# Hybrid encoder trunk: both mixing stages in a new order, small parameters loaded first, and two additions of each state-space tile moved from VectorE to GpSimd

## The chip, the cores and the metric

The kernel runs on one core of a Trainium2 chip. The time is the device time of one execution in microseconds (us). The five engines of the core run side by side, each through its own instruction stream in order: TensorE (PE, matrix products into PSUM banks), VectorE (DVE), ScalarE (ACT), GpSimd (POOL) and SyncE (SP, which here only starts DMAs). They wait for one another by semaphores.

## The reference

The input is 256 tokens of 1024 features, in float32. After a layer norm come two layers. Each has a token mixer and then a channel mixer, and each ends with a residual sum and a layer norm. The channel mixer is a dense SwiGLU in layer 0 and a top-2-of-8 mixture of experts in layer 1.

The token mixer projects the tokens once and hands the columns to four head groups of 256 features: retention, S5 (a diagonal state-space model), Hyena (gated long convolutions, whose filters come from a small sine network) and mLSTM. Their outputs are concatenated and projected. The S5 part is

```python
bu = einsum("gpc,blgc->blgp", b_bar[direction], ug)
_, states = associative_scan(combine, (decay, bu), reverse=reverse, axis=1)   # a_bar is complex
return einsum("gcp,blgp->blgc", c[direction], states).real
y = run(0, False) + run(1, True) + d_skip * u
z = gelu(y);  out = z * sigmoid(z @ w_glu)
```

## The kernel before

The kernel is written by hand, engine by engine. Each engine's part has a function `mix_0` for the mixer of layer 0 and `mix_1` for that of layer 1, which list the calls in the order in which that engine runs them. Nothing is planned by a program: the lists are the schedule. Between the two mixers stands the dense channel mixer (products at L1030 and L1040), and behind the second one the experts (L1145, L1172), which take up the time from about 600 us to the end.

**The projection.** The input projection is cut into 12 units (`unit`, L616). Unit 0 gives the S5 inputs, units 1 to 3 the Hyena columns, 4 and 5 the query and key columns of the mLSTM, 6 and 7 those of retention, 8 to 11 the remaining ones. Each is 8 or 16 products over the 1024 features (L640 or L648). `UNITS` gives their order and `WIN_LOADS` the weight transfers that bring them in pairs. Units 4 and 5 come last before the change. The output projection (`out_product`, L846) accumulates four banks over the four head groups.

**The state-space tiles.** The complex scan is made real by rotating the inputs by the phase of each state and back. There are eight tiles of 128 states, each with both directions, and per tile these steps:

- TensorE: `s5_in` (L784) multiplies B and the inputs into one PSUM bank, real and imaginary halves. It uses 32 rows of the array.
- VectorE: `s5_tile_products` (L2009, L2010) multiplies a table of cosines and sines by the two halves of the bank: two instructions of 1024 elements per partition, one input in SBUF, the other in PSUM. The scratch tiles are `p1` and `p2`.
- VectorE: `s5_tile_scan` first completes the rotation (an addition at L2019 and a subtraction at L2020, 512 elements, both inputs in SBUF), then runs four scans of 256 elements (L2025, L2027).
- VectorE: `s5_tile_rotate` (L2038, L2039, L2041) turns the states back.
- GpSimd: adds the two parts (L521, 1024 elements), straight after the rotation. When four tiles are done TensorE multiplies them by C (`s5_y`, L807).

**The other work on VectorE.** In layer 0 VectorE and ScalarE also build the tables (`pre(0, 13)` to `pre(0, 20)`, one for each tile, L1822 to L1830), the S5 constants (`s5_angle`, `pre(0, 11)`, `pre(0, 12)`) and the Hyena filters (`pre(0, 0)` to `pre(0, 6)`; TensorE's part at L587 and L600). In layer 1 all of that is done during the dense channel mixer, and the tables are loaded. `conv` (L1837, L1842) is the short convolution, `rotary`, `ml_rows_a`, `ml_rows_b`, `hyena_product`, `hyena_gate` (L1889, L1893), `ret_decay` and `ret_norm` serve the other groups.

**The tail.** After retention's head norm the mLSTM is left: `ml_mask` (L1958), an exponential on ScalarE, `ml_weights`, `ml_out` on TensorE for each of four heads, then `ml_norm`, `head_scale(1)`, a transpose (`head_out`, L688) and the last output products. In both layers the first `ml_mask` of VectorE marks the start of this tail.

**Parameters.** `pr` holds the small parameters and the weights of one layer, 1728 KB, loaded by one DMA (SP, L416) behind the inputs, the norm weights, the identity and the first weights of the projection. The semaphore `s_par` covers all of it.

`link` makes VectorE wait for its own last result before the next instruction.

## Time and profile before

| | us |
|---|---|
| median of 3 runs | 1611.61 (1609.13 to 1612.51) |
| the profiled execution | 1607.81 |
| its span | 1606.0 |

The times of engines over the span: PE 1562.5 busy (97%), DVE 1337.2 (83%), ACT 963.7 (60%), POOL 47.1 (3%). A busy PE isn't a PE at its peak, since its records overlap. The page cuts the span into 40 slices; each digit is a share in tenths:

```profile
PE   7998999999999899999999999999999999999997
DVE  6999567766498867889989998988998989898897
ACT  3321455644212346777777677677777777777775
POOL 0112000000021100000000000000000000000000
PEclk9998999999999999999999999999999999999999
```

A slice is 40 us. The mixer of layer 0 fills slices 1 to 5, that of layer 1 the end of slice 11 to slice 15. POOL works in these two only.

### The profile page before, as it was taken

To read this page: it belongs to the slowest core of one execution; us is meant where nothing else is said; L and a number is where in the kernel's file an instruction comes from. 1 tells how busy PE (TensorE), PEld (TensorE's weight loads), DVE (VectorE), ACT (ScalarE), POOL (GpSimd) and SP (SyncE) were. 2 spreads that over 40 slices of the span, in tenths; PEclk is the share of its full clock that TensorE was granted. 3 is DMA by queue.
4 is the path that set the end of the run, shared out by engine and by line. 5 is a ranking of instruction groups with operands and counts; after the bars stand their busy time and mean duration, and the time that the engine had idled before them with its cause. 6 is when DMAs were issued, how large, how long until landed. Compare 5 with 4: busy or idle time off the path is not lost.

```text
span 1606.0 us, 18396 instructions
## 1 busy us (share of the span) xinstructions
PE 1562.5 (97%) x7492; PEld 1235.9 (77%) x7492; DVE 1337.2 (83%) x1435; ACT 963.7 (60%) x1000; POOL 47.1 (3%) x34
## 2 busy tenths in 40 slices
PE   7998999999999899999999999999999999999997
PEld 5656679988766667888888888888888788888885
DVE  6999567766498867889989998988998989898897
ACT  3321455644212346777777677677777777777775
POOL 0112000000021100000000000000000000000000
PEclk9998999999999999999999999999999999999999
DMA  8231445644424156999889999989899989999981
GB/s 334 105 133 52 157 159 231 245 174 171 193 105 142 61 230 274 372 369 379 342 341 370 355 369 371 354 333 372 345 378 373 348 343 368 380 361 373 365 338 52
DMA packets 41676, 446.33 MB, mean 278 GB/s; under 512 B 4457, under 2 KB 4585, under 8 KB 8433
## 3 DMA queue, kind: packets, MB, share of 16 engines
q1 hardware_dynamic: 39360, 438.78, 70.2%
q10 hardware_dynamic: 2224, 6.31, 1.1%
q8 instruction: 61, 1.00, 0.2%
q14 instruction: 31, 0.25, 0.0%
HBM read 439.81 MB, written 5.26 MB: 277 GB/s over the span
## 4 chain that ended last, share of the span: by engine, by line
PE 80%; DVE 13%; ACT 4%; issue 1%; DMA 1%; POOL 0%; SPq 0%; DVEq 0%; ACTq 0%
PE bank L1145 35%; PE bank L1172 16%; PE bank L1030 8%; PE bank L640 4%; PE bank L1040 4%; PE bank L648 3%; PE bank L846 3%; DVE ring_lo L2198 2%; PE bank L1153 1%; DVE ring_lo L2340 1%; ACT ex_up_hi L1498 1%; PE bank L1093 1%; DMA pr<-par 1%; PE bank L1116 1%; ACT ex_w_hi L1624 1%
## 5 line engine op out<-in xcount | busy, mean ns | idle before, releaser
L2198 DVE TENSOR_TENSOR ring_lo<-ring,ex_up_hi 128x2048 fp32r<-128x2048 f32 x224 | 512.9, 2290 | 51.3 <-ACT ex_up_hi L1498 49.8
L1498 ACT ACTIVATE ex_up_hi<-ring 128x2048 fp32r<-128x2048 f32 x224 | 429.2, 1916 | 105.9 <-PE bank L1145 105.9
L1145 PE MATMUL bank<-ex_up_hi,ex_x_hi 128*128 128x512 f32 x896 | 362.6, 405 | 5.6 <-DVE ring_lo L2198 4.7
L1145 PE MATMUL bank<-ring_lo,ex_x_hi 128*128 128x512 f32 x896 | 350.7, 391 | 0.0
L1145 PE MATMUL bank<-ex_up_hi,ex_x_lo 128*128 128x512 f32 x896 | 349.7, 390 | 0.0
L2340 DVE TENSOR_TENSOR ring_lo<-ring,ex_w_hi 128x2048 fp32r<-128x2048 f32 x111 | 253.2, 2281 | 0.0
L1624 ACT ACTIVATE ex_w_hi<-ring 128x2048 fp32r<-128x2048 f32 x111 | 211.5, 1905 | 0.0
L1145 PEld LDWEIGHTS bank<-ex_up_hi,ex_x_hi 128*128 128x128 f32 x896 | 168.3, 188 | 43.8 <-DVE ring_lo L2198 12.3
L1145 PEld LDWEIGHTS bank<-ring_lo,ex_x_hi 128*128 128x128 f32 x896 | 168.2, 188 | 36.7
L1145 PEld LDWEIGHTS bank<-ex_up_hi,ex_x_lo 128*128 128x128 f32 x896 | 168.8, 188 | 30.5
L1172 PE MATMUL bank<-ex_w_hi,ex_mid_hi 128*128 128x512 f32 x448 | 174.5, 389 | 0.0
L1172 PE MATMUL bank<-ring_lo,ex_mid_hi 128*128 128x512 f32 x448 | 174.3, 389 | 0.0
L1172 PE MATMUL bank<-ex_w_hi,ex_mid_lo 128*128 128x512 f32 x448 | 174.3, 389 | 0.0
L1172 PEld LDWEIGHTS bank<-ex_w_hi,ex_mid_hi 128*128 128x128 f32 x448 | 84.1, 188 | 17.7 <-DVE ring_lo L2340 0.3
L1172 PEld LDWEIGHTS bank<-ring_lo,ex_mid_hi 128*128 128x128 f32 x448 | 84.1, 188 | 17.5
L1172 PEld LDWEIGHTS bank<-ex_w_hi,ex_mid_lo 128*128 128x128 f32 x448 | 84.1, 188 | 17.4
L1030 PE MATMUL bank<-ff_x_hi,ff_up_hi 128*128 128x256 f32 x336 | 96.1, 286 | 0.0
L1030 PE MATMUL bank<-ff_x_hi,ff_up_lo 128*128 128x256 f32 x336 | 95.1, 283 | 0.0
L1030 PE MATMUL bank<-ff_x_lo,ff_up_hi 128*128 128x256 f32 x336 | 95.1, 283 | 0.0
L1618 ACT ACTIVATE sc<-bank 128x256 f32<-128x256 f32 x112 | 43.0, 384 | 84.2 <-PE bank L1145 84.2
L648 PE MATMUL bank<-win,hT 128*128 128x512 f32 x192 | 93.4, 619 | 0.0
L640 PE MATMUL bank<-hT,win 128*128 128x256 f32 x384 | 85.4, 381 | 3.1 <-ACT hT L1247 1.6
(355 smaller groups left out, 2028.1 us busy)
## 6 DMA issues: line engine op xcount, KB each, us to landing
ring<-moe SPq DMA_DIRECT2D x112, 2048.0 KB, 7.6
ring<-moe SPq DMA_DIRECT2D x112, 1024.0 KB, 7.4
ring<-ffn SPq DMA_DIRECT2D x11, 3072.0 KB, 11.1
win<-w_in SPq DMA_DIRECT2D x12, 2048.0 KB, 8.6
win<-w_out SPq DMA_DIRECT2D x4, 2048.0 KB, 10.2
lnb<-ln SPq DMA_DIRECT2D x4, 1024.0 KB, 5.7
tab<-yT ACTq DMA_DIRECT2D x8, 512.0 KB, 5.5
pr<-par SPq DMA_DIRECT2D x2, 1728.0 KB, 11.1
```

The lines of the kernel that those rows point to most:

```text
L640: ins = mm(b[:, half * L:(half + 1) * L], w[:, k, c:c + P], hT[:, k, :], start=(k == 0), stop=(k == KT - 1))
L648: ins = mm(b[:, :], x, w[:, k, :], start=(k == 0), stop=(k == KT - 1))
L846: ins = mm(bank[b][:, :], yT[:, k, t * P:(t + 1) * P], w[:, k, :], start=(n == 0 and i == 0), stop=(n == 3 and i == 1))
L1030: ins = mm(bank[4 + u % 2][:, w * L:(w + 1) * L], (ff_up if u else ff_up_first)[j][:, w, k, :], ff_x[i][:, k, :], start=(k == 0 and n == 0 ...
L1040: ins = mm(bank[2 * t + hf][:, :], ff_mid[i][:, u % 2, t * P:(t + 1) * P], w2[j][:, hf * 512:(hf + 1) * 512], start=False, stop=(u == NU - ...
L1145: ins = mm(b[:, :], ex_x[x % 3][x_][:, k, :], (ex_up_hi, lo)[w_][:, k, :], start=(k == 0 and m == 0), stop=(k == KT - 1 and m == 2))
L1172: ins = mm(bank[2 * (x % 2) + hf][:, :], ex_mid[a][:, g % 2, f * P:(f + 1) * P], w2[b], start=(c == 0 and f == 0 and m == 0), stop=(c == N ...
L1498: act(ex_up_hi[:, HS * q:HS * (q + 1), :], wt[:, HS * q:HS * (q + 1), :], ACT.Copy).then_inc(e_uh, 1)
L1618: act(sil[g % 2], bank[4 + g % 2][:, 0:L], ACT.Silu).then_inc(e_sil, 1)
L1624: act(ex_w2_hi[g % 2][:, :], ring[here][:, UPW:SLOT], ACT.Copy).then_inc(e_wh, 1)
L2198: tt(ring_lo[s][:, half], ring[s][:, half], hi.bitcast(F32), ALU.subtract).then_inc(e_ul, 1)
L2340: tt(ring_lo[s][:, UPW:SLOT], ring[s][:, UPW:SLOT], ex_w2_hi[g % 2][:, :].bitcast(F32), ALU.subtract).then_inc(e_wl, 1)
```

## The change

- GpSimd does the addition and subtraction of L2019 and L2020. Its loop now runs nine times: in turn `i` it waits for the products of tile `i`, completes them, and only then sums the rotated states of tile `i - 1`. VectorE's scan waits for the new semaphore `b_in`.
- `s5_in` serves several tiles in one call, each into a bank of its own (four at once in layer 1, two and two in layer 0), and alternates between the row groups of the array.
- The second and third layer of the filter network use both halves of the rows: the weights `hy_w2` and `hy_w3` are laid out twice and side by side, and the products of one token tile come in pairs. The squares of the filters in layer 0 are added on VectorE first (`square_total(0)`), so that TensorE needs 4 products in place of 16 for the norm.
- The columns of `pr` from `gate_b` on (the S5 constants, biases and norm weights) come in a DMA of their own, before all others, with the semaphore `s_small`. The small constants (`cst`, behind the identity) come before the first projection weights; the rest of `pr` comes behind these. `s5_angle(0)` on VectorE and `s5_step(0)`, `s5_radius(0)`, `pre(0, 11)` on ScalarE move ahead of the first layer norm.
- The units run in the order 0, 8, 9, 10, 11, 1 to 7, always through banks 5 and 6, and all engines have new lists in both mixers. The semaphores of the weight slots for the dense and expert parts are merged into one for each slot.

```diff
-UNITS = (0, 8, 9, 10, 11, 1, 2, 3, 6, 7, 4, 5)
+UNITS = (0, 8, 9, 10, 11, 1, 2, 3, 4, 5, 6, 7)
 POS = {u: p for p, u in enumerate(UNITS)}
-UNIT_BANK = (5, 6, 5, 6, 5, 6, 5, 6, 5, 6, 1, 2)
 VW = H * (HD + 1)
-WIN_LOADS = ((0, (0, 3)), (1, (8, 9)), (2, (10, 11)), (1, (1, 2)), (2, (6, 7)), (0, (4, 5)))
+WIN_LOADS = ((0, (0, 1)), (1, (8, 9)), (2, (10, 11)), (1, (2, 3)), (0, (4, 5)), (2, (6, 7)))
...
-    ("s5_c", 2 * 16 * 32), ("s5_b", 512), ("glu", 512), ("hy_w3", 1024), ("hy_w12", 64), ("gate_w", KT * 16),
+    ("s5_c", 2 * 16 * 32), ("s5_b", 512), ("glu", 512), ("hy_w3", 960), ("hy_w12", 128), ("gate_w", KT * 16),
...
-        fx_ = [[a[0:64, i * 256:(i + 1) * 256] for i in range(4)] for a in work]
+        fx_ = [[a[:, i * 256:(i + 1) * 256] for i in range(4)] for a in work]
...
 
+        def s5_bank(l, i):
+
+            if l:
+                return i if i < 4 else 3
+            return 2 + i % 2 if i < 4 else 3
...
                     sp.wait_ge(f_pm, 2)
-                    sp.wait_ge(f_sq, 4)
+                    sp.wait_ge(f_sq, 5)
                 elif n == 4:
...
                 sp.dma_start(ln_home(n), ln[n]).then_inc(s_ln, 16)
 
+            few = PAR["gate_b"][0]
+            sp.dma_start(pr[:, few:PAR_W], par[0, :, few:PAR_W]).then_inc(s_small, 16)
             for t in range(TT):
                 sp.dma_start(h[:, t, :], x[t * P:(t + 1) * P, :]).then_inc(s_x[t], 16)
             load_ln(0)
             first = slice(*CONST["ident"])
             sp.dma_start(cst[:, first], const[:, first]).then_inc(s_id, 16)
+            sp.dma_start(cst[:, first.stop:CONST_W], const[:, first.stop:CONST_W]).then_inc(s_pos, 16)
...
                 ins.then_inc(ml_ones, 1)
-                for i in range(8):
-                    po.wait_ge(b_x, 2 * (8 * l + i + 1))
-                    T = s5_table(i)
-                    nc.gpsimd.tensor_tensor(T, T, s5_work[2 + i % 2], ALU.add).then_inc(b_sum, 1)
+                p1, p2 = s5_work[0:2]
+                for i in range(9):
+                    if i < 8:
+                        po.wait_ge(b_p, 8 * l + i + 1)
+                        nc.gpsimd.tensor_tensor(p1[:, 0], p1[:, 0], p2[:, 1], ALU.add).then_inc(b_in, 1)
+                        nc.gpsimd.tensor_tensor(p2[:, 0], p2[:, 0], p1[:, 1], ALU.subtract).then_inc(b_in, 1)
+                    if i:
+                        po.wait_ge(b_x, 2 * (8 * l + i))
+                        T = s5_table(i - 1)
+                        nc.gpsimd.tensor_tensor(T, T, s5_work[2 + (i - 1) % 2], ALU.add).then_inc(b_sum, 1)
                 for m in range(2):
...
-                elif k < 6:
-                    j = k - 2
-                    if j == 0:
+                    mm(pb[1][:, 0:L], W("hy_w12", 64), fx[3][0:64], start=True, stop=True).then_inc(f_mm, 1)
+                elif k in (3, 5):
+                    pass
                         pe.wait_ge(f_sin, 2 * l + 2)
-                    if j >= 2:
-                        pe.wait_ge(f_win, 4 * l + j - 1)
-                    mm(pb[j % 2][:, :], fx[3][:, (j // 2) * P:(j // 2 + 1) * P],
-                       W("hy_w3", 64)[:, (j % 2) * 512:(j % 2 + 1) * 512], start=True, stop=True).then_inc(f_raw, 1)
+                    else:
+                        pe.wait_ge(f_win, 4 * l + 2)
+                    for o in range(2):
+                        r = slice(64 * o, 64 * o + 64)
+                        mm(pb[o][:, :], fx[3][r, t * P:(t + 1) * P], W("hy_w3")[r, 0:512],
+                           start=True, stop=True).then_inc(f_raw, 1)
                 elif k == 6:
-                    if l:
-                        pe.wait_ge(f_sq, 5)
-                        terms = [(0, 0)]
-                    else:
-                        pe.wait_ge(f_win, 4)
-                        pe.wait_ge(f_sq, 2)
-                        terms = [(t, d) for t in range(TT) for d in range(2)]
+                    pe.wait_ge(f_sq, 3 * l + 3)
                     for j in range(4):
                         o, c = j // 2, j % 2
-                        for i, (t, d) in enumerate(terms):
-                            ins = mm(pb[0][:, 2 * j:2 * j + 2], fsq[t][:, o, d, c * P:(c + 1) * P], K("ones")[:, 0:2],
-                                     start=(i == 0), stop=(i == len(terms) - 1))
+                        ins = mm(pb[0][:, 2 * j:2 * j + 2], fsq[0][:, o, 0, c * P:(c + 1) * P], K("ones")[:, 0:2],
+                                 start=True, stop=True)
...
-            def s5_in(l, i):
-
-                if i == 0:
+            def s5_in(l, first, n):
+
+                if first == 0:
                     pe.wait_ge(s_par, 16 * (l + 1))
                     pe.wait_ge(u_ev, l + 1)
                 else:
-                    pe.wait_ge(b_p, 8 * l + i)
-                r = 32 * (i % 4)
+                    pe.wait_ge(b_p, 8 * l + first)
                 for s in range(2):
-                    ins = mm(bank[3][:, s * L:(s + 1) * L], s5b[r:r + 32, i // 4, s, :],
-                             uT[r:r + 32, i // 4, :], start=True, stop=True)
-                ins.then_inc(b_mm, 1)
+                    for i in range(first, first + n):
+                        r = 32 * (i % 4)
+                        ins = mm(bank[s5_bank(l, i)][:, s * L:(s + 1) * L], s5b[r:r + 32, i // 4, s, :],
+                                 uT[r:r + 32, i // 4, :], start=True, stop=True)
+                        if s:
...
-            def square_total():
-
-                fsq = fsq_[1]
-                ve.wait_ge(f_sq, 4)
+            def square_total(l):
+
+                fsq = fsq_[l]
+                ve.wait_ge(f_sq, 3 * l + 2)
...
                 p1, p2 = s5_work[0:2]
-                ve.wait_ge(b_p, v + 1)
-
-                tt(p1[:, 0], p1[:, 0], p2[:, 1], ALU.add)
-                link(tt(p2[:, 0], p2[:, 0], p1[:, 1], ALU.subtract))
```

VectorE's list in layer 0, and below it the part of layer 1 from tile 4 on (tiles 0 to 3 stay as they were: products, scan and rotation one after the other, with `gates(1)` before the second rotation):

```diff
             def mix_0():
-                s5_angle(0)
                 pre(0, 11)
-                pre(0, 12)
                 pre(0, 13)
                 pre(0, 14)
                 pre(0, 15)
+                ve.wait_ge(ht_ready, 4)
+                pre(0, 12)
+                s5_tile_products(0, 0)
+                s5_tile_scan(0, 0)
                 pre(0, 16)
+                s5_tile_rotate(0, 0)
                 pre(0, 17)
-                s5_tile_products(0, 0)
+                s5_tile_products(0, 1)
                 pre(0, 18)
-                s5_tile_scan(0, 0)
-                gates(0)
-                s5_tile_rotate(0, 0)
-                pre(0, 19)
-                pre(0, 20)
-                s5_tile_products(0, 1)
                 s5_tile_scan(0, 1)
                 s5_tile_rotate(0, 1)
                 pre(0, 0)
+                gates(0)
                 s5_tile_products(0, 2)
+                s5_tile_scan(0, 2)
                 pre(0, 1)
-                conv(0, 1)
-                s5_tile_scan(0, 2)
-                conv(0, 2)
                 s5_tile_rotate(0, 2)
                 s5_tile_products(0, 3)
+                pre(0, 19)
+                pre(0, 20)
+                s5_tile_scan(0, 3)
+                conv(0, 1)
+                s5_tile_rotate(0, 3)
+                conv(0, 2)
+                s5_tile_products(0, 4)
                 pre(0, 2)
-                conv(0, 3)
-                s5_tile_scan(0, 3)
                 pre(0, 3)
-                s5_tile_rotate(0, 3)
                 pre(0, 4)
-                s5_tile_products(0, 4)
                 pre(0, 5)
                 s5_tile_scan(0, 4)
+                square_total(0)
+                s5_tile_rotate(0, 4)
+                conv(0, 3)
+                conv(0, 4)
+                s5_tile_products(0, 5)
                 pre(0, 6)
-                s5_tile_rotate(0, 4)
                 pre_norm(0)
-                ml_rows_a(0)
-                rotary(0, 6)
-                s5_tile_products(0, 5)
-                ml_rows_b(0)
-                rotary(0, 7)
                 s5_tile_scan(0, 5)
                 s5_tile_rotate(0, 5)
                 s5_tile_products(0, 6)
+                ml_rows_a(0)
+                s5_tile_scan(0, 6)
+                ml_rows_b(0)
+                conv(0, 5)
+                s5_tile_rotate(0, 6)
+                s5_tile_products(0, 7)
+                hyena_product(0, 0)
                 ml_cols(0)
-                hyena_product(0, 0)
-                s5_tile_scan(0, 6)
+                s5_tile_scan(0, 7)
+                rotary(0, 6)
+                rotary(0, 7)
+                hyena_gate(0, 0)
+                s5_tile_rotate(0, 7)
                 ret_decay(0, 0)
                 ret_decay(0, 1)
-                s5_tile_rotate(0, 6)
-                s5_tile_products(0, 7)
-                hyena_gate(0, 0)
-                s5_tile_scan(0, 7)
-                s5_tile_rotate(0, 7)
+                hyena_product(0, 1)
                 ret_decay(0, 2)
                 ret_decay(0, 3)
-                hyena_product(0, 1)
+                s5_skip(0)
                 ret_norm(0)
-                s5_skip(0)
-                conv(0, 4)
+                hyena_gate(0, 1)
                 head_scale(0)
-                conv(0, 5)
-                hyena_gate(0, 1)
                 ml_mask(0, 0)
                 ml_mask(0, 1)
-                s5_end(0)
                 ml_weights(0, 0)
                 ml_weights(0, 1)
                 ml_mask(0, 2)
+                ml_mask(0, 3)
                 ml_weights(0, 2)
-                ml_mask(0, 3)
+                s5_end(0)
                 ml_weights(0, 3)
                 ml_norm(0)
...
                 s5_tile_scan(1, 4)
                 s5_tile_rotate(1, 4)
                 conv(1, 2)
+                s5_tile_products(1, 5)
                 conv(1, 3)
+                s5_tile_scan(1, 5)
                 ml_rows_a(1)
-                s5_tile_products(1, 5)
-                hyena_product(1, 0)
-                ml_rows_b(1)
-                rotary(1, 6)
-                hyena_gate(1, 0)
-                ml_cols(1)
-                s5_tile_scan(1, 5)
                 s5_tile_rotate(1, 5)
                 s5_tile_products(1, 6)
-                rotary(1, 7)
-                hyena_product(1, 1)
-                ret_decay(1, 0)
+                ml_rows_b(1)
+                conv(1, 4)
+                conv(1, 5)
                 s5_tile_scan(1, 6)
                 s5_tile_rotate(1, 6)
+                hyena_product(1, 0)
+                ml_cols(1)
+                s5_tile_products(1, 7)
+                rotary(1, 6)
+                s5_tile_scan(1, 7)
+                rotary(1, 7)
+                hyena_gate(1, 0)
+                s5_tile_rotate(1, 7)
+                ret_decay(1, 0)
                 ret_decay(1, 1)
-                s5_tile_products(1, 7)
-                conv(1, 4)
-                s5_tile_scan(1, 7)
-                s5_tile_rotate(1, 7)
+                hyena_product(1, 1)
                 ret_decay(1, 2)
                 ret_decay(1, 3)
-                hyena_gate(1, 1)
-                conv(1, 5)
                 s5_skip(1)
                 ret_norm(1)
+                hyena_gate(1, 1)
                 head_scale(2)
+                s5_end(1)
                 ml_mask(1, 0)
-                s5_end(1)
+                ml_mask(1, 1)
                 ml_weights(1, 0)
-                ml_mask(1, 1)
                 ml_weights(1, 1)
                 ml_mask(1, 2)
+                ml_mask(1, 3)
                 ml_weights(1, 2)
-                ml_mask(1, 3)
                 ml_weights(1, 3)
                 ml_norm(1)
```

TensorE in layer 0 runs `s5_in(0, 0, 2)` behind unit 0, `s5_in(0, 2, 2)` behind unit 10, and one tile at a time from the fifth on. `pre(0, 6)`, with its new wait for `square_total(0)`, stands ahead of unit 5, `pre(0, 7)` to `pre(0, 10)` inside it. Units 6 and 7 come last, and behind them `hyena_inverse(0, 0)`, retention, `s5_y(0, 1)` and the output products. In layer 1 `s5_in(1, 0, 4)` stands in the middle of unit 8, as `s5_in(1, 0)` did.

## Rows read from the trace of the kernel before

**Rows 1.** Windows by stage: span, busy us (instructions) of PE, PEld, DVE, ACT, POOL; clock; DMA.
```profile
36.00:174.20 138.20, 131.55 (x551) 87.89 (x550) 124.90 (x197) 40.38 (x66) 20.50 (x9) 0.93 0.23 84
174.20:213.80 39.60, 36.81 (x135) 19.21 (x135) 23.08 (x57) 17.29 (x39) 1.65 (x1) 1.00 0.60 231
438.40:557.40 119.00, 113.62 (x524) 77.55 (x524) 105.11 (x164) 25.71 (x42) 20.56 (x9) 1.00 0.27 98
557.40:594.30 36.90, 36.79 (x129) 19.86 (x130) 23.50 (x56) 15.63 (x35) 1.65 (x1) 0.95 0.52 200
```
**Rows 2.** DVE's waits, layer 0 mixer (36 to 174.2 us): total, times, longest.
```profile
DVE cv L1837 <- ACT cv L1311: 9.9, 3, 4.4
```
**Rows 3.** DVE's waits, layer 1 mixer (438 to 557.4 us).
```profile
DVE cv L1837 <- ACT cv L1311: 7.1, 3, 4.0
DVE ring L1930 <- ACT ring L1350: 2.7, 1, 2.7
DVE lnb L1910 <- POOL small L524: 1.8, 1, 1.8
```
**Rows 4.** Timeline of DVE, layer 1, tile 0: start, us, instruction.
```profile
438.40 1.22 DVE L2009 TENSOR_TENSOR ring<-ring,bank 128x1024 f32<-128x1024 f32 x1 [14.78 <-PE bank L793]
...
440.79 0.69 DVE L2019 TENSOR_TENSOR ring<-ring 128x512 f32<-128x512 f32 x1
...
442.11 1.27 DVE L2025 TENSOR_TENSOR_SCAN ring<-small,ring 128x256 f32<-128x256 f32 x2
...
447.17 1.22 DVE L2009 TENSOR_TENSOR ring<-ring,bank 128x1024 f32<-128x1024 f32 x1
```
**Rows 5.** POOL's instructions by line: busy, mean ns, idle before.
```profile
L521 POOL TENSOR_TENSOR ring<-ring 128x1024 f32<-128x1024 f32 x16 | 37.8, 2359 | 231.0 <-DVE ring L2041 231.0
```
**Rows 6.** Single DVE lines: duration in ns, least/median/most.
```profile
L1760 DVE TENSOR_SCALAR sc<-sc x2: 284/1126/1967, 61.6 to 67.8; 64x256 f32<-64x256 f32 x2
L1822 DVE TENSOR_SCALAR yT<-cst,small x16: 341/349/2543, 26.9 to 50.8; 128x256 f32<-128x256 f32 x16
L1930 DVE TENSOR_SCALAR ring<-ring x2: 416/1436/2457, 105.6 to 496.5; 4x512 f32<-4x512 f32 x2
L1893 DVE TENSOR_TENSOR yT<-cv x2: 691/704/717, 173.4 to 546.8; 128x512 f32<-128x512 f32 x2
```
**Rows 7.** Timeline of POOL and DVE: two sums, and what ran beside the second.
```profile
105.42 2.35 POOL L521 TENSOR_TENSOR ring<-ring 128x1024 f32<-128x1024 f32 x1 [10.12 <-DVE ring L2041]
...
544.59 2.36 POOL L521 TENSOR_TENSOR ring<-ring 128x1024 f32<-128x1024 f32 x1 [8.64 <-DVE ring L2041]
...
546.78 0.72 DVE L1893 TENSOR_TENSOR yT<-cv 128x512 f32<-128x512 f32 x1
```
**Rows 8.** Timeline of DVE at the start; idle time before and its releaser in brackets.
```profile
17.94 0.17 DVE L1748 TENSOR_TENSOR small<-pr,small 128x16 f32<-128x16 f32 x1 [4.22 <-ACT small L1255]
...
20.94 0.18 DVE L1785 TENSOR_TENSOR small<-small 128x16 f32<-128x16 f32 x1 [2.11 <-ACT small L1283]
...
23.04 0.69 DVE L1805 TENSOR_TENSOR yT<-pr,small 128x512 f32<-128x512 f32 x1
...
26.90 0.62 DVE L1822 TENSOR_SCALAR yT<-cst,small 128x256 f32<-128x256 f32 x2
...
28.74 0.62 DVE L1822 TENSOR_SCALAR yT<-cst,small 128x256 f32<-128x256 f32 x2
...
36.02 1.21 DVE L2009 TENSOR_TENSOR ring<-ring,bank 128x1024 f32<-128x1024 f32 x1
```
**Rows 9.** Timeline of SP at the start: the norm's DMA.
```profile
1.66 0.42 SPq L408 DMA_DIRECT2D lnb<-ln  x1
```
**Rows 10.** Timeline of DVE: a short convolution (its first half).
```profile
163.20 0.87 DVE L1837 SCALAR_TENSOR_TENSOR cv<-bank,pr,cv 128x255 f32<-128x255 f32 x2 [4.36 <-ACT cv L1311]
```
**Rows 11.** Timeline of PE: 64-row products, in one row group and in two by turns.
```profile
176.78 1.13 PE L760 MATMUL bank<-cv 64*128 64x256 f32 x8
...
348.06 1.12 PE L587 MATMUL bank<-pr,cv 64*128 64x512 f32 x2
```

296 lines of the change are left out of this document (152 added, 144 removed).

## The prediction

> **What bounds the kernel now.** I began with the chain of waits over the whole span, to see which part belongs to TensorE alone. The dense part and the experts are a chain of PE products, and the change gives them almost nothing. What it touches is the two mixers, so I cut these out as windows [rows 1]. In the mixer of layer 0, from the first product of a state-space tile to the first `ml_mask`, DVE is busy for 124.9 of 138.2 us, and PE's clock is granted at 0.93: PE has to wait often enough to lose it, and DVE sets the pace. In layer 1 the two are closer: PE is busy for 113.6 of 119.0 us, DVE for 105.1. There DVE's own waits [rows 3] are mostly for columns that PE hasn't projected yet. Behind the first `ml_mask` both layers run a tail of fixed length, 39.6 and 36.9 us [rows 1]: four heads of mLSTM, its norm, the last output products. So the question for each mixer is when DVE reaches that mask. The timeline of DVE, POOL and PE inside the windows gives the prices.
>
> **What POOL does to DVE.** This decides the case. In three places a TENSOR_SCALAR of DVE runs beside POOL's sum, and takes 1967, 2543 and 2457 ns where the same line otherwise takes 284, 349 and 416 [rows 6]. It waits until POOL is done; the three stalls are 5.9 us. The products of a tile, one input in SBUF and one in PSUM, run beside the sum at their usual 1.22 us [rows 4]. An instruction with both inputs in SBUF meets the sum just once: L1893 begins at 546.78, POOL ends at 546.95 [rows 7], and that instance takes 717 ns, against 691 for the same line elsewhere [rows 6]. The TENSOR_SCALARs come free some 0.14 us before POOL's recorded end (L1930 from 105.6 for 2457 ns, less its usual 416, is 107.6; that sum ends at 107.8 [rows 7]), and 546.95 less 0.14 less 546.78 is 0.03 us: what L1893 has lost. One instance of 26 ns is thin, but it is the only row, and it says that two SBUF inputs are held back as well. The scans (L2025), the rotation (L2038 to L2041), `pre(0, 6)` and `ml_rows_b` are all of that kind.
>
> The Trainium skill says the same, and it speaks against this change: in SBUF — State Buffer, section "Who interferes with whom", a DVE instruction with two SBUF inputs contends with a GpSimd instruction that reads SBUF, and whichever comes second is blocked whole. By that page the sum is the first one below; without it, by the products' row alone, it would be the rival's.
>
> **The change, part by part.**
>
> *Two instructions leave DVE.* From L2019 to the first scan is 1.32 us [rows 4], eight tiles a layer: 10.6 us less of DVE in each.
>
> *What takes their place.* The scan now waits for POOL. Its price for 512 elements isn't shown. The nearest row is its own 1024-element sum, 2359 ns [rows 5]; half of that, 1.18, is the lower end, the whole of it the upper. I take 1.23, since time per element is what the larger one mostly shows, and 0.1 for the two hand-overs: 2.56 us a tile (2.4 to 4.8), 20.5 a layer. Behind the waiting scan stands all of DVE's list. What DVE does between products and scan can cover it only where it has an input in PSUM. In layer 0 that is `pre(0, 2)` to `pre(0, 5)` and the first four instructions of `hyena_product(0, 0)`, each time four of 0.6 us, 4.9 together. The other fillers there are TENSOR_SCALARs. In layer 1 it is `conv(1, 1)` and `conv(1, 3)` at 1.7 (two halves of 0.87, [rows 10]), the start of `rotary(1, 6)` at 1.3, and I give 1.5 for `conv(1, 4)` and `conv(1, 5)`: 6.2. Tiles 0 to 3 of layer 1 have nothing between.
>
> *The sum moves.* Before, it started with the rotation's end and lay beside the next tile's products, which it leaves alone. Now it comes behind POOL's new pair, and so beside the scans of the next tile. If these are held back, it costs 2.36 us for each tile but the last: 16.5 a layer. If not, nothing.
>
> *The start.* DVE waits 4.2 us, until 17.9, for the parameters by way of ScalarE, and 2.1 for ScalarE's sines [rows 8]. With the small ones first, both waits hide in front of and behind the first norm. One more DMA issue (0.42 us, [rows 9]) delays the norm by 0.4. So: norm done at 17.9 - 4.2 + 0.4 = 14.1; `pre(0, 11)` 2.1; three tables at 1.84, 5.5; `pre(0, 12)` 3.9 (which needs the large rest of `pr`, due by then); first products at 25.6 in place of 36.0 [rows 8]. Two tables less are done by then, 3.7 us, to be made up later. If the small block came no earlier, the two waits would stay: 6.3 us.
>
> *Layer 0 from first products to mask.* Before 138.2: 124.9 busy, 10.7 of waits, nearly all for `conv` [rows 2], 2.6 between instructions. DVE's own work after: 124.9 + 2.6 - 5.9 (stalls, counted anew below) - 10.6 + 3.7 + 1.9 (`square_total(0)`, by 1.22 and 0.69 [rows 4]) = 116.6. With POOL: + 20.5 + 16.5 - 4.9 = 148.7. The waits for `conv` go, since units 4 and 5 come early; late next is PE's Hyena and retention work, which stands behind `pre(0, 6)` and its new wait. I allow 2. The mask is then at 25.6 + 150.7 = 176.3, against 174.2: **+2.1**.
>
> *Layer 1.* Before 119.0: 105.1 busy, 11.6 waits [rows 3], 2.3 between. After: 105.1 + 2.3 - 10.6 + 1.8 (POOL's power, still waited for) + 0.7 (`s5_end` ahead of the mask) = 99.3; + 20.5 + 16.5 - 6.2 = 130.1: **+11.1**. The first products stay where they were, as `s5_in` keeps its place. PE would need less than 113.6, so it isn't the bound any more.
>
> *Nothing on the path, while DVE is it:* `s5_in` in several banks, the paired filter products and the shorter norm sum in the mixers, the new order of PE's units, the merged semaphores. PE gains a few us that it then waits. If DVE's cover is gone (the rival below), they count.
>
> *The dense part* is PE's chain, and there layer 1's filter products are on it. Two of 64 rows and 512 columns took 1.12 us as one product alone; products that alternate between row groups, 8 records of 256, took 1.13 [rows 11], half as long per column. Four products become two pairs: **-2.1**, between 0 and -2.3.
>
> The tails keep their length. Sum: 2.1 + 11.1 - 2.1 = +11.1 us. On the profiled execution's 1607.8 that gives 1618.9. The three runs have their median 3.8 above it, so the forecast for the median is 1611.6 + 11 = **1622**.
>
> **Rivals.**
>
> *Nothing is held back but TENSOR_SCALAR* (chance 0.15). For it: the products' rows; the only row against it is 26 ns. Then each tile pays only the uncovered part of 2.56. Layer 1: 4 x 2.56 for tiles 0 to 3, 2.2 for the rest, 99.3 + 12.4 = 111.7, -7.3. Layer 0: 116.6 + 11.7 + 3 for TENSOR_SCALARs that now meet POOL's pair and sum = 131.3, mask at 156.9, of which PE's own work (131.6 us busy before, [rows 1]) gives back some 3: -14. With -2.1, 1611.6 - 23 = 1588. It turns to the slower side when more than about half of the 33 us of sums lands on DVE.
>
> *The sum loses its turn* (0.10). If DVE's scans, back to back, keep POOL out, the sum falls beside the next products, as before. The 16.5 goes in both layers: layer 1 at -5, layer 0 at -12, 1592. Against it: the stalled L1822 began 0.04 us ahead of POOL and still waited.
>
> *The small parameters don't land ahead of the norm* (0.05): the block is one of short rows. 6 us on top of the forecast, 1628.
>
> **From these to the numbers.** The forecast has 0.70, with its own range 1607 to 1636: the pair's price and the sum's cover can each move it by 8. A measurement here tells 0.2%, 3.2 us. Inside the forecast I put 0.10 below 1608.4, 0.10 within 3.2 us of before and 0.50 above. Faster is 0.15 + 0.10 + 0.10 = 0.35, the same 0.10, slower 0.50 + 0.05 = 0.55. The range must reach to the two faster cases, or it leaves out 0.25: 1588 to 1636.
>
> **What would show it.** First products near 25.6 us, and not 36. POOL with pairs near 1.2 us each. In layer 1 the start of one tile's products to the next: 8.77 before [rows 4], 12.4 from tile 1 on if the sums hold DVE back, 10.0 if not; the two middle scans' durations tell which, one of them near 3 us or all near 0.68. Masks near 176 and 568. The forecast is wrong if the scans keep their time beside a sum, or if a sum lies beside products.

## The result, and the profile after

In nine runs each the changed kernel takes 1614.35 us (1613.37 to 1616.79) and the one before 1611.56 us (1607.46 to 1612.80); the ratio is 1.0027, 95% interval 1.0017 to 1.0036. So it is slower, by 4.4 us by the ratio and by 2.8 between the medians. I had forecast slower, but by 10, at 1622 us. The profiled executions differ by 6.0 us of span, 1606.0 before and 1612.0 after, and that is the number to set against the forecast's sum of 11.1, which was made for the profiled execution. The profiled run of before lay 3.8 us under its median, that of after 0.6 under its own; that explains why the medians lie closer together than the spans.

Windows of the changed kernel, cut at the same events as [rows 1] (columns as there): first products to first mask of layer 0, from there to the first split input of the dense part, on to the first products of layer 1, to its first mask, and to its first residual addition.

```profile
25.82:176.33 150.51, 134.26 (x572) 87.74 (x570) 131.86 (x191) 45.68 (x73) 42.40 (x25) 0.93 0.26 101
176.33:218.40 42.07, 39.55 (x153) 22.01 (x152) 26.40 (x65) 17.95 (x42) 1.65 (x1) 1.00 0.54 217
218.40:435.90 217.50, 216.26 (x1450) 193.39 (x1450) 137.16 (x208) 115.81 (x161) 1.20 (x4) 1.00 0.53 204
435.90:565.40 129.50, 116.06 (x509) 78.71 (x509) 110.51 (x148) 25.38 (x42) 41.19 (x25) 0.96 0.25 90
565.40:595.52 30.12, 29.82 (x122) 16.79 (x121) 19.72 (x48) 15.40 (x33) 1.65 (x1) 1.00 0.63 236
```

The same cuts in the trace of before and in three kernels of the experiments give a table that adds up to the spans (us, each the length of a window):

| stage | before | after | forecast of the change | measured | only the pair moved | sum first | pair back |
|---|---|---|---|---|---|---|---|
| start to first products | 36.0 | 25.8 | -10.4 | -10.2 | 36.7 | 26.0 | 25.9 |
| layer 0, products to mask | 138.2 | 150.5 | +12.5 | +12.3 | 153.2 | 139.9 | 141.1 |
| its tail, to the dense part's input | 44.2 | 42.1 | 0 | -2.2 | 47.4 | 42.1 | 42.3 |
| dense part, to layer 1's products | 219.9 | 217.5 | -2.1 | -2.4 | 219.9 | 217.5 | 217.5 |
| layer 1, products to mask | 119.0 | 129.5 | +11.1 | +10.5 | 131.9 | 115.9 | 113.9 |
| its tail, to the residual | 31.9 | 30.1 | 0 | -1.8 | 30.6 | 30.1 | 30.1 |
| the rest | 1016.7 | 1016.5 | 0 | -0.2 | 1016.8 | 1016.4 | 1016.3 |

The price of GpSimd's pair is at the first tile. Timeline of VectorE and GpSimd there:

```profile
25.82 1.22 DVE L2027 TENSOR_TENSOR ring<-ring,bank 128x1024 f32<-128x1024 f32 x1
...
28.25 1.26 POOL L535 TENSOR_TENSOR ring<-ring 128x512 f32<-128x512 f32 x1 [18.88 <-DVE ring L2028]
...
30.78 0.69 DVE L2040 TENSOR_TENSOR_SCAN ring<-small,ring 128x256 f32<-128x256 f32 x1 [2.60 <-POOL ring L536]
```

The price of the sum is at tile 1 of layer 1, the counterpart of [rows 4]. Timelines of VectorE, then GpSimd:

```profile
445.93 1.22 DVE L2027 TENSOR_TENSOR ring<-ring,bank 128x1024 f32<-128x1024 f32 x1
...
450.88 3.40 DVE L2040 TENSOR_TENSOR_SCAN ring<-small,ring 128x256 f32<-128x256 f32 x2 [2.60 <-POOL ring L536]
...
458.17 1.22 DVE L2027 TENSOR_TENSOR ring<-ring,bank 128x1024 f32<-128x1024 f32 x1
```
```profile
448.36 1.27 POOL L535 TENSOR_TENSOR ring<-ring 128x512 f32<-128x512 f32 x1 [7.53 <-DVE ring L2028]
...
450.80 2.35 POOL L540 TENSOR_TENSOR ring<-ring 128x1024 f32<-128x1024 f32 x1
```

The sum begins at 450.80, 0.08 us ahead of the scans, and the first two scans last 3.40 us where they need 1.27; the next two, when the sum is over, have their usual 1.24. The tile takes 458.17 - 445.93 = 12.24 us. Before, it took 456.04 - 447.17 = 8.87, from the start at the end of [rows 4] to this one (the difference, 3.37, is the pair's 1.24 and the sum's 2.13):

```profile
456.04 1.22 DVE L2009 TENSOR_TENSOR ring<-ring,bank 128x1024 f32<-128x1024 f32 x1
```

Scans are held in this way in tiles 1 to 5 of layer 1, 3.40 us each time, and in only one tile of layer 0, tile 2. In the other tiles fillers stand between products and scans, and GpSimd's instructions hold those (last section).

### The profile page after: what moved, and what is told of

Same layout as the page of the kernel before. It is cut to its first block, busy times and chain, and to the rows that moved or that the text cites. A ratio compares the mean times of both kernels' runs of the same rounds, so it can differ in the third digit from the quotient of the medians.

```text
span 1612.0 us, 18353 instructions
## 1 busy us (share of the span) xinstructions
PE 1550.3 (96%) x7468; PEld 1229.5 (76%) x7468; DVE 1345.6 (83%) x1405; ACT 964.8 (60%) x1001; POOL 89.6 (6%) x66
## 4 chain that ended last, share of the span: by engine, by line
PE 75%; DVE 11%; ACT 4%; issue 1%; POOL 1%; DVEq 0%
PE bank L1154 35%; PE bank L1181 16%; PE bank L1039 8%; PE bank L1049 4%; PE bank L862 3%; DVE ring_lo L2214 2%; PE bank L1162 1%; DVE ring_lo L2357 1%; ACT ex_up_hi L1508 1%; PE bank L1102 1%; PE bank L662 1%; PE bank L683 1%; PE bank L1125 1%; ACT ex_w_hi L1637 1%; DVE ring L2040 1%
## 5 line engine op out<-in xcount | busy, mean ns | idle before, releaser
L1154 PEld LDWEIGHTS bank<-ex_up_hi,ex_x_lo 128*128 128x128 f32 x896 | 168.8, 188 | 30.4
L654 PE MATMUL bank<-hT,win 128*128 128x256 f32 x384 | 89.9, 394 | 7.3 <-DVE cv L1860 5.6
```

Source lines behind the costliest of these rows:

```text
L654: ins = mm(b[:, half * L:(half + 1) * L], w[:, k, c:c + P], hT[:, k, :], start=(k == 0), stop=(k == KT - 1))
L1154: ins = mm(b[:, :], ex_x[x % 3][x_][:, k, :], (ex_up_hi, lo)[w_][:, k, :], start=(k == 0 and m == 0), stop=(k == KT - 1 and m == 2))
```

## The experiments

Theory: what costs is GpSimd's work on SBUF. The pair costs 1.24 us a tile where nothing covers it (2.56 forecast for it, less the 1.32 that VectorE saves), and the sum costs 2.13 us because it now lies beside scans, whose inputs are both in SBUF. Rivals: the new order of TensorE's units and of the fillers; GpSimd simply having too much to do. And for what the forecast missed: the tails don't have a fixed length.

**The sum ahead of the pair.** In the changed kernel's GpSimd loop:

```
                 for i in range(9):
+                    if i: (wait, sum of tile i-1)
                     if i < 8: (wait, add and subtract of tile i)
-                    if i: (wait, sum of tile i-1)
```

> The changed kernel with one thing other: GpSimd takes the sum of tile i-1 ahead of the pair of tile i, in place of behind it. The instructions are the same in number and size. Theory (a GpSimd instruction on SBUF and a VectorE instruction with two SBUF inputs shut each other out, products with a PSUM input go free): the sum now lies beside the products of the next tile, which take 2.44 us, and is done (2.36) when they end, so the pair isn't late. Scans 1.27 us for the two where they took 3.40, tile to tile in layer 1 10.0 us where it was 12.13. That is 2.13 x 7 = 14.9 us of VectorE in each layer; but TensorE was busy for 134.3 of 150.5 us and 116.1 of 129.5, so it becomes the bound: layer 0 from products to mask about 139, layer 1 about 119, in all -18 to -24 against the changed kernel, near 1593 us. Rival (the scans are long because they follow a hand-over from GpSimd, or GpSimd's two jobs a tile are simply too much work for it): scans stay long or the pair comes 2.4 us later, tiles stay at 12 us or grow, time 1614 or above.

Measured: 1590.48 us, ratio to before 0.9884 (0.9868 to 0.9901). VectorE and GpSimd in layer 1:

```profile
435.55 1.22 DVE L2027 TENSOR_TENSOR ring<-ring,bank 128x1024 f32<-128x1024 f32 x1
...
440.50 1.27 DVE L2040 TENSOR_TENSOR_SCAN ring<-small,ring 128x256 f32<-128x256 f32 x2 [2.60 <-POOL ring L540]
...
445.66 1.22 DVE L2027 TENSOR_TENSOR ring<-ring,bank 128x1024 f32<-128x1024 f32 x1
```
```profile
435.60 2.36 POOL L536 TENSOR_TENSOR ring<-ring 128x1024 f32<-128x1024 f32 x1 [5.14 <-DVE ring L2056]
...
439.21 1.26 POOL L540 TENSOR_TENSOR ring<-ring 128x512 f32<-128x512 f32 x1
```

Products keep 1.22 us beside a sum, scans are back at 1.27, the wait for the pair is 2.60 as in the changed kernel, and from one tile's products to the next it is 10.11 us; what is left above 8.87 is the pair's 1.24. The same instructions on the same engines, in another order, are 24 us of span faster (1612.0 to 1588.0), and VectorE is busy for 8.1 us less in layer 0 (123.8 in place of 131.9) and 13.2 less in layer 1 (97.3 in place of 110.5). The rival of an overloaded GpSimd is out.

**The pair back on VectorE**, all else of the change kept:

```
-                ve.wait_ge(b_in, 2 * v + 2)
+                ve.wait_ge(b_p, v + 1)
+                tt(p1[:, 0], p1[:, 0], p2[:, 1], ALU.add)
+                link(tt(p2[:, 0], p2[:, 0], p1[:, 1], ALU.subtract))
```

> The changed kernel with the pair (add and subtract of 512 elements a partition) back on VectorE, and GpSimd with nothing but the sum, begun as soon as the rotation ends, beside the next products. All else of the change stays: small parameters first, new order, state-space inputs in several banks, paired filter products. Theory (the pair on GpSimd is what costs, the rest gains): VectorE gives back 1.24 us a tile of waiting and 2.13 us a tile of held-back scans, so by VectorE alone 25 us a layer where nothing covered them; TensorE then sets the end, at no less than its busy 134 and 116 us. Layer 0 from products to mask 137, layer 1 117; -20 to -28 against the changed kernel, near 1590 us, some 20 below the kernel before. Rival (the new order of TensorE's units and of the fillers is what costs, the pair is nearly covered): no more than 5 us are won back, time 1609 to 1614.

Measured: 1589.79 us, ratio 0.9882 (0.9865 to 0.9899). The rest of the change gains 18.8 us of span (1606.0 to 1587.2), and the pair on GpSimd gives away 24.8 (1587.2 to 1612.0): 9.4 in layer 0, 15.6 in layer 1. The layout isn't what costs. The two versions end within 0.8 us of each other although VectorE is busy for 105.4 us in layer 1 in this one and for 97.3 in the one with the sum first: TensorE, busy for 111.2 of 113.9 us, has become the bound.

**Only the pair moved**, in the kernel before:

```
+                        nc.gpsimd.tensor_tensor(p1[:, 0], p1[:, 0], p2[:, 1], ALU.add)
+                        nc.gpsimd.tensor_tensor(p2[:, 0], p2[:, 0], p1[:, 1], ALU.subtract)
                         (behind them the sum of tile i-1)
```

> The kernel before with only the pair moved to GpSimd, and the sum behind the next tile's pair, as the changed kernel has them; order, start and banks are those of before. Theory: each tile pays 2.56 - 1.32 = 1.24 us and 2.13 us where the scans meet the sum, 27 us a layer at most; in layer 0 10.7 us of waits for convolution inputs and in layer 1 11.6 us of waits take up a part, and the three held-back TENSOR_SCALARs (5.9 us) change places. +8 to +18 in layer 0, +10 to +16 in layer 1, time 1630 to 1645. Tile 0 to tile 1 in layer 1 10.0 us, then 12.1, where before they were 8.77. Rival (the move is harmless, the mixers got longer by the new order alone): within 5 us of before.

Measured: 1636.65 us, ratio 1.0168 (1.0151 to 1.0185). Layer 0 gets 15.0 us longer and layer 1 12.9; both tails change too, by +3.2 and -1.3, and these two are TensorE's clock (see the runs with less work below). In the order of before the move costs 30.6 us of span, of which the tails are 1.9, in the new one 24.8. In layer 0 it is 15.0 against 9.4. That the new order's fillers cover the difference isn't shown: there the version with the pair on VectorE is near TensorE's own work (133.4 of 141.1 us busy), which hides a part of what the pair costs. In layer 1, where the new order alone would be at 113.9 us, the move costs more (12.9 against 15.6).

**Half a sum**, in the changed kernel:

```
-    nc.gpsimd.tensor_tensor(T, T, s5_work[2 + (i - 1) % 2], ALU.add)
+    nc.gpsimd.tensor_tensor(T[:, 0], T[:, 0], s5_work[2 + (i - 1) % 2][:, 0], ALU.add)
```

> The changed kernel with GpSimd's sum over 512 of its 1024 elements a partition; the order stays. What it leaves out: the sum of the other half, so the states of one sign are incomplete. Theory (the scan is held back for as long as the GpSimd instruction lasts, less the 0.23 us by which the sum had begun or is released early): the sum takes 1.25 us, the first two scans 1.27 + 1.0 = 2.3 us where they took 3.40, and tile to tile in layer 1 is 11.0 us where it was 12.13. Rival (a fixed price for each meeting of the two engines, whatever the length): scans stay at 3.4 and tiles at 12.1.

Timeline of VectorE, then GpSimd, tile 1 of layer 1:

```profile
439.73 1.22 DVE L2027 TENSOR_TENSOR ring<-ring,bank 128x1024 f32<-128x1024 f32 x1
444.68 2.32 DVE L2040 TENSOR_TENSOR_SCAN ring<-small,ring 128x256 f32<-128x256 f32 x2 [2.60 <-POOL ring L536]
...
450.88 1.22 DVE L2027 TENSOR_TENSOR ring<-ring,bank 128x1024 f32<-128x1024 f32 x1
```
```profile
444.61 1.27 POOL L540 TENSOR_TENSOR ring<-ring 128x512 f32<-128x512 f32 x1
```

Scans 2.32 us, 11.15 from products to products. The hold-back is 1.05 us for a sum of 1.27 and 2.13 for one of 2.35: it follows GpSimd's length, less 0.22 both times. Of the 0.22 the sum has 0.07 to 0.08 behind it when the scans begin, so the scans come free some 0.14 us ahead of its recorded end, the 0.14 that the prediction read from the TENSOR_SCALARs. The one run took 1600.12 us; layer 1 took 122.0 us, about half of the way from 129.5 to 115.9. There is no fixed price for a meeting.

**The small parameters late**, in the changed kernel (and with them the angles on VectorE and step sizes on ScalarE behind the norm):

```
-            sp.dma_start(pr[:, few:PAR_W], par[0, :, few:PAR_W]).then_inc(s_small, 16)
             ...
             load_win(0, 0)
+            sp.dma_start(pr[:, few:PAR_W], par[0, :, few:PAR_W]).then_inc(s_small, 16)
```

> The changed kernel with its start undone: the small parameters are issued behind the first weights, just ahead of the large rest, and the step sizes, angles and sines that need them come behind the first norm on VectorE and ScalarE, as before. All else of the change stays. Theory (the wait for the parameters, 4.2 us, and that for the sines, 2.1 us, come back, less 0.4 for the DMA issue; VectorE is the bound of layer 0 in the changed kernel, so it passes on whole): first products at 31.7 in place of 25.8, first mask 5.9 later, +5.9 in all. Rival (TensorE projects on meanwhile and the waits for it in layer 0, 6 us of VectorE's, shrink): first products at 31.7 but the mask only 1 to 3 us later.

Waits on VectorE's timeline, the counterparts of [rows 8]:

```profile
16.73 0.17 DVE L1764 TENSOR_TENSOR small<-pr,small 128x16 f32<-128x16 f32 x1 [2.71 <-ACT small L1267]
...
31.09 1.22 DVE L2027 TENSOR_TENSOR ring<-ring,bank 128x1024 f32<-128x1024 f32 x1
```

First products 5.3 us later (31.09 against 25.82), the first mask 4.8 (181.11 against 176.33), the span 5.1. The two runs had their median at 1620.80 us, ratio 1.0071 (1.0049 to 1.0093), where the changed kernel had 1.0027. The block came somewhat sooner than in the kernel before, so the wait was 2.71 and not 4.2; that for the sines was 2.11 as before. What the start loses passes on nearly whole, as the theory has it; the rival of 1 to 3 is out.

**Less work in TensorE's tail.** In the changed kernel and in the kernel before:

```
-                for i, k in enumerate(GROUPS[group]):
+                for i, k in enumerate(GROUPS[group] if (l, group, b) not in
+                                      ((0, "ret", 1), (1, "s5", 1)) else ()):
```

> The changed kernel without one group of output products in each layer (retention into quarter 1 in layer 0, state space into quarter 1 in layer 1, 1.85 us of TensorE each, both in front of the transposes of the last head norm). What it leaves out: these two contributions to the mixers' outputs. My prediction's step (behind the first mask a tail of fixed length, set by the mLSTM heads and their norm on VectorE): the residual additions come when they did, 0 us. Rival (from the first output product on, TensorE's own list of products sets the end; in the changed kernel the norm is ready 2.1 us before TensorE reaches its transposes): 1.85 us earlier in each layer, -3.7 in all.

> The kernel before without the same two groups of output products as in the run of the changed kernel without them (retention into quarter 1 in layer 0, state space into quarter 1 in layer 1). What it leaves out: these two contributions. There TensorE waited 1.18 us for the last norm in layer 0, and reached its transposes 0.43 us after the norm in layer 1. Theory (the tail is the longer of two chains: mLSTM and its norm on VectorE from the mask on, or TensorE's list from the first output product on): the last residual additions of layer 0 come when they did, those of layer 1 0.4 us earlier, where the changed kernel gave 1.1 and 1.7. Rival (TensorE's list alone sets the tail in both kernels): 1.1 to 1.85 earlier in both layers here too.

In the changed kernel (one run, 1613.51 us) the first residual addition came 1.71 us sooner after the mask in layer 0 (29.64 against 31.35) and 1.72 in layer 1 (28.40 against 30.12), near the rival's 1.85. The forecast's fixed tail is out: TensorE's list sets it there. (Of the 1.71 only 1.07 reached the dense part's input, since VectorE then waited 1.04 us for the norm weights' DMA. The span gained only 0.3, since the last thousand us, which the edit doesn't touch, took 1018.3 where they took 1016.5.)

In the kernel before (one run, 1612.39 us) layer 0's tail became 5.0 us longer (49.2), which neither theory had. TensorE's timeline in that run:

```profile
184.55 1.85 PE L760 MATMUL bank<-cv 64*128 64x256 f32 x8 [0.43 <-DVE sc L1973]
...
188.95 3.28 PE L846 MATMUL bank<-win,yT 128*128 128x512 f32 x4
...
208.10 0.66 PE L688 MATMUL bank<-cst,lnb 128*128 128x128 f32 x4 [2.90 <-DVE lnb L1911]
208.60 12.16 PE L846 MATMUL bank<-win,yT 128*128 128x512 f32 x24
```

TensorE waited 2.90 us for the norm where it had waited 1.18, as a shorter list in front of the same norm would have it. But the 5.0 us are clock. From 184.55 on TensorE ran for some 7 us at granted clocks of 0.60 and 0.54 (4 us windows from 184 and 188), and four products took 3.28 us in place of 1.94: 3.3 of the 5.0 us were lost by there. The products that the edit leaves out would stand only behind the last `ml_out`, so up to this point TensorE has the same list as in the kernel before, with the same waits of 0.95 and 0.43. The other 1.7 are the 24 products behind the norm, 12.16 us in place of 10.47, at a granted clock of 0.59 in the 4 us from 208. The run that moves only the pair has all its products and the first of these dips too (0.66 and 0.50 in the windows from 197 and 201), and that is its +3.2:

```profile
198.46 2.08 PE L766 MATMUL bank<-cv 64*128 64x256 f32 x8 [0.43 <-DVE sc L1979]
```

So in layer 0 this run doesn't tell the two theories apart by the tail's length; only the longer wait speaks for the two chains. In layer 1 the tail became 1.55 us shorter (30.38) where I expected 0.4. The profiled execution of the kernel before had a clock dip there (next section). Against 30.57 in the run that moves only the pair, which has the same list and no dip, it is 0.2 shorter, with TensorE waiting 1.18 us for the norm: near the theory's 0.4 and far from the rival's 1.1 to 1.85.

**A version from the findings.** Sum first, and the pair on GpSimd only where fillers cover it:

```
+        def pair_on_pool(l, i):
+            return l == 0 and i not in (0, 2)
```

> A version meant to beat both kernels. The changed kernel with GpSimd's sum ahead of its pair, and the pair on VectorE wherever VectorE has nothing to do beside it: all of layer 1, and tiles 0 and 2 of layer 0; six tiles of layer 0 keep it on GpSimd, under fillers. Theory (a pair on GpSimd costs 1.24 us where nothing covers it and gains 1.32 us of VectorE where fillers do; the sum is free beside products): layer 0 from products to mask 1 to 2.5 us below the 139.9 of the run with the sum first, layer 1 at 113.9 as with the pair back on VectorE, span 1584 to 1586, median near 1587. Rival (TensorE is the bound in layer 0, where it was busy for 130.6 of 139.9 us at a clock of 0.96): layer 0 stays at 139.9 and only layer 1 gains, span 1586 to 1587.

Measured: 1588.33 us, ratio 0.9874 (0.9857 to 0.9890). Layer 0 took 139.7 and layer 1 113.9, the rival's numbers: in layer 0 the two pairs gave nothing. (The span, 1585.5, lay in the theory's range all the same.) Then two steps of TensorE's list in layer 0 were moved to close two waits:

```
                 s5_in(0, 2, 2)
-                pre(0, 1)
                 unit(0, 11, 0)
                 unit(0, 11, 1)
+                pre(0, 1)
...
+                unit(0, 5, 1)
                 s5_in(0, 6, 1)
                 pre(0, 7)
                 ...
-                unit(0, 5, 1)
```

> The hybrid version with two steps of TensorE's list in layer 0 moved: the second layer of the filter network behind the whole of unit 11, and the second half of unit 5 ahead of the state-space inputs of tile 6 and the filter spectra. In the hybrid TensorE waited there for 2.56 and 2.78 us, and in the 5 us behind each wait its granted clock was 0.66 and 0.76. Theory (a wait of TensorE costs its own length and then the lower clock, some 1.5 us more, and VectorE waits 2.6 to 3 us three times in this layer for what TensorE and ScalarE deliver late): layer 0 from products to mask 136 to 138 in place of 139.7, median near 1585.5. Rival (VectorE, busy for 126.4 of 139.7 us, is the bound of this layer in either order, and TensorE's waits are only what VectorE leaves it): 139 to 140, no difference.

> The hybrid version once more, beside the run with the two moved steps, on the same chip. Both theories: span 1585 to 1587, layer 0 from products to mask 139.7 within 0.5.

Measured on one chip: 1588.81 us with the steps moved (ratio 0.9867, 0.9850 to 0.9883) and 1589.43 without (0.9877, 0.9861 to 0.9894). Windows of products to mask, layer 0 and layer 1, of the first, and of the second:

```profile
26.46:163.50 137.04, 129.29 (x572) 84.93 (x571) 126.99 (x194) 45.77 (x73) 36.57 (x21) 0.99 0.29 108
423.08:539.91 116.83, 114.11 (x508) 77.90 (x509) 105.39 (x164) 25.46 (x42) 20.57 (x9) 0.97 0.27 99
```
```profile
26.09:165.85 139.76, 132.87 (x572) 86.49 (x570) 126.41 (x194) 45.77 (x73) 36.56 (x21) 0.95 0.29 108
425.43:540.21 114.78, 112.61 (x508) 77.21 (x509) 105.38 (x165) 25.59 (x42) 20.59 (x9) 0.99 0.28 101
```

Layer 0 is 2.7 us shorter with TensorE's clock at 0.99 instead of 0.95, and VectorE does the same work in it (127.0 and 126.4 us). That is the theory's number, and it speaks against the rival (VectorE as bound), but it is one execution, and the theory's path to it isn't what happened: the two waits are gone, others came (one of 2.82 us), and TensorE's idle time in the window rose from 6.9 to 7.8 us. What fell is its busy time for the same 572 products, from 132.9 to 129.3, at the higher clock. And layer 1, whose instructions are the same in both, took 116.8 at a clock of 0.97 in that execution, 114.8 at 0.99 in this and 113.9 at 1.00 in the first hybrid run, so 2.7 us is within what the clock does from one execution to the next. The median forecast, 1585.5, was missed, and the two medians can't be told apart. Both beat the kernel before by 1.2 to 1.3%; which of the four fast versions is best stays open.

## Why the prediction had the direction right and the size wrong

*The pair's price: right.* 2.56 us a tile was forecast, the wait is 2.60 where nothing stands in between. The lower end of the bounds (half of the 1024-element sum, [rows 5]) was nearly the price: 1.26.

*Scans are held by the sum: right, and with it the direction.* It was taken from 26 ns in one row [rows 7]. A held tile costs 2.13 us in place of 2.36. But it is six tiles and not fourteen: 12.8 us of the forecast's 33. The rest of what GpSimd held back were fillers. The Trainium skill (SBUF — State Buffer, "Who interferes with whom") had named a VectorE instruction with two SBUF inputs as one that contends with a GpSimd instruction that reads SBUF, and one with at most one SBUF input, outside of the 2-port modes, as free. Scans at 3.40 against 1.27 us and products at 1.22 beside a sum agree on both sides.

*The stages.* Start, layer 0 to its mask, dense part and layer 1 to its mask came out at -10.2, +12.3, -2.4 and +10.5 against -10.4, +12.5, -2.1 and +11.1. First masks at 176.33 and 565.40. In layer 0 this is luck, two errors that cancel. The forecast's 150.7 has 15.6 us of waits for the pair (20.5 less 4.9) and 2 of other waits; VectorE waited 5.2 for the pair, in two tiles, and 11.1 for others, 2.8, 3.3 and 2.6 among them. Fillers covered the pair also where they were to cover nothing, and were held themselves (last section); VectorE's busy time came to 131.9 against 130.5 in the forecast. In layer 1 the terms hold better: 12.2 us of waits for the pair against 14.3, 5.2 of others against 1.8, busy for 110.5 against 111.7.

*The failed step: "Behind the first `ml_mask` both layers run a tail of fixed length".* It holds 4.0 of the missing 5.1 us (-2.2 and -1.8 where I put 0). In layer 0 the mask is the wrong anchor: the tail ends when both TensorE's list of output products and the norm are through. In layer 1 nearly all of it is TensorE's clock in the one execution that the forecast was built on. Timeline of TensorE in the kernel before, layer 0 and then layer 1:

```profile
180.78 1.52 PE L780 MATMUL bank<-vo,sc 128*128 128x65 f32 x12 [0.95 <-DVE sc L1973]
182.72 1.13 PE L760 MATMUL bank<-cv 64*128 64x256 f32 x8 [0.43 <-DVE sc L1973]
...
202.99 0.66 PE L688 MATMUL bank<-cst,lnb 128*128 128x128 f32 x4 [1.18 <-DVE lnb L1911]
203.48 10.47 PE L846 MATMUL bank<-win,yT 128*128 128x512 f32 x24
...
552.75 1.99 PE L817 MATMUL bank<-ring,pr 128*128 128x256 f32 x8 [1.80 <-ACT ring L1393]
...
557.51 0.88 PE L688 MATMUL bank<-cst,sc 128*128 128x128 f32 x4 [1.70 <-DVE sc L1911]
558.18 5.11 PE L846 MATMUL bank<-win,yT 128*128 128x512 f32 x8
```

and in the changed kernel, layer 0 and layer 1:

```profile
178.05 5.42 PE L862 MATMUL bank<-win,yT 128*128 128x512 f32 x12 [0.93 <-ACT yT L1352]
...
191.53 12.23 PE L862 MATMUL bank<-win,yT 128*128 128x512 f32 x28
203.60 0.60 PE L702 MATMUL bank<-cst,lnb 128*128 128x128 f32 x4
...
563.58 1.98 PE L862 MATMUL bank<-win,yT 128*128 128x512 f32 x4
```

Before, TensorE waits three times in layer 0's tail once its output products have begun, 2.56 us together; after, not once between 178.05 and the last output product. It has the same 64 products to do in each, so its waits are what the tail can save. That the pairs of heads in `ml_mask` and `ml_out` save them is argued from the lists; no run takes them alone. 1.55 of the 2.2 us are there at the first residual addition (32.90 to 31.35 us behind the mask). The other 0.6 comes behind it, where 20 products are left in place of 24. This part is shown by the rows and by the changed kernel's run with less work.

In layer 1 the eight products at 558.18 took 5.11 us, behind waits of 1.80 and 1.70. The run that moves only the pair has the same list, and there they took 3.60 behind the same two waits:

```profile
589.32 0.66 PE L694 MATMUL bank<-cst,sc 128*128 128x128 f32 x4 [1.70 <-DVE sc L1917]
589.81 3.60 PE L852 MATMUL bank<-win,yT 128*128 128x512 f32 x8
```

That is 1.5 us of lower clock, in this execution of the kernel before and in no other traced tail of layer 1. The two other runs of that order have no dip in this tail, which lasts 30.6 and 30.4 us (the second with four products fewer); the changed kernel's lasts 30.1. So 1.4 to 1.5 of the 1.8 us are no saving by the change, and the forecast of no change there would have been off by some 0.3 to 0.5 from an execution without the dip.

*The rest.* Another 1.1 us of the five is in terms of 0.2 to 0.6, of which only the start went against me. And the forecast was carried from a profiled run to the median by adding the sum to the median. That run was among the fastest of its kernel and the one of the changed kernel lay near its median, and that makes another 3.2 us: from 1622.7 to 1614.35 it is 8.3, of which 5.1 are the sum's. Where a usual execution of the kernel before spends the 3.8 us that the profiled one didn't isn't shown, since only one was traced.

*The rivals.* The faster ones are out by the scans of layer 1; the version with the sum first is what the second of them describes, and it took 1590.5 us where I put 1592. The last (small parameters not early) would have cost 5.1 us, where I put 6.

## What to carry to other kernels

When work is handed from VectorE to GpSimd, its own price can be the smaller part; look at what the new order of GpSimd's list puts beside instructions with two SBUF inputs. Put GpSimd's long instructions beside those that read PSUM, and they hold nothing back. Take as the anchor of a tail the engine whose list ends last, with its waits, not the event that looks like its start. And before a stage of one execution goes into a sum, look at its granted clock: a dip in it may not come again.

## What the runs showed of the hardware

Fillers beside GpSimd are held not once but by turns. In layer 0 of the changed kernel GpSimd runs pair and sum from 41.70 to 46.77 without a gap, and VectorE has three short instructions of a table there:

```profile
41.54 1.62 DVE L1840 TENSOR_SCALAR yT<-cst,small 128x256 f32<-128x256 f32 x2
43.19 1.37 DVE L1843 TENSOR_SCALAR yT<-yT 128x512 f32<-128x512 f32 x1
44.59 2.72 DVE L1848 TENSOR_TENSOR yT<-yT 128x512 f32<-128x512 f32 x1
```
```profile
41.70 1.31 POOL L535 TENSOR_TENSOR ring<-ring 128x512 f32<-128x512 f32 x1 [10.96 <-DVE ring L2028]
42.97 1.31 POOL L536 TENSOR_TENSOR ring<-ring 128x512 f32<-128x512 f32 x1
44.24 2.53 POOL L540 TENSOR_TENSOR ring<-ring 128x1024 f32<-128x1024 f32 x1
```

They take 5.71 us in place of 1.74 (0.62, 0.43 and 0.69 in the run with late parameters, where GpSimd is idle), each held by another GpSimd instruction, while GpSimd's own grow only from 1.26 to 1.31 and from 2.35 to 2.53 (elsewhere in this run to 1.71 and 2.80). A stream of short VectorE instructions isn't cover for a stream on GpSimd; they give it one turn each.

The same short waits of TensorE are followed by a lower clock in some executions and not in others. In the 4 us windows from 556 and 560 of the kernel before, with the waits of 1.80 and 1.70 in front, the granted clock was 0.73 and 0.85, between the levels of 1.2 and 2.4 GHz; with the same two waits in the run that moves only the pair it was 1.00 in that tail throughout. Behind waits of 0.95 and 0.43 in layer 0's tail it is the other way about: 1.00 in the kernel before, 0.60 and 0.54, or 0.66 and 0.50, in two other runs, at a price of 3.2 to 3.3 us. And with identical instructions layer 1 of the last three runs took 113.9, 114.8 and 116.8 us at clocks of 1.00, 0.99 and 0.97. What decides it isn't shown.
